# Feed-forward of a two-block transformer kernel: the up half leaves PSUM times the gate, and the norm's factor is applied to the down projection's result

## The reference

```python
def rmsnorm(x, g):
    y = x * rsqrt(mean(x * x, axis=-1) + 1e-6)       # one factor for each token
    return y * g

# first block
h2 = rmsnorm(x, norm_ffn_g[l])
x = x + (silu(h2 @ w_gate[l]) * (h2 @ w_up[l])) @ w_down[l]

# each layer of the stack
def _swiglu(x, w_in, w_out):
    gu = x @ w_in
    return (silu(gu[..., :2816]) * gu[..., 2816:]) @ w_out
x = x + _swiglu(_rmsnorm(x, g_ffn[i]), w_ffn_in[i], w_ffn_out[i])
```

## Time and profile before

| | us |
|---|---|
| median of 3 runs | 3124.99 (3124.5 to 3125.08) |
| span of the profiled execution, first to last instruction | 3122.7 |
| PE busy | 3103.8 (99%) |
| DVE busy | 1538.4 (49%) |
| ACT busy | 987.3 (32%) |
| POOL busy | 50.9 (2%) |
| mean granted clock of PE | 0.997 of full |

### The profile page before, as it was taken

One profiled execution on the slowest core, in us unless ns is written; L12 is line 12 of the kernel. 1 busy time (PEld: TensorE's weight loads), 2 busy tenths in 40 slices (PEclk: granted clock), 3 DMA queues, 4 the chain that ended last, 5 costly groups with the idle time before them and its releaser, 6 DMA issues.

```text
span 3122.7 us, 36149 instructions
## 1 busy us (share of the span) xinstructions
PE 3103.8 (99%) x14981; PEld 2572.7 (82%) x14981; DVE 1538.4 (49%) x1632; ACT 987.3 (32%) x1090; POOL 50.9 (2%) x149
## 2 busy tenths in 40 slices
PE   9999999999999999999999999999999999999998
PEld 7878888888888888888888888888888888888887
DVE  7975443464444443467544434655442454454433
ACT  3463221344442222344322222323222344332213
POOL 5100000000000000000000000000000000000000
PEclk9999999999999999999999999999999999999999
DMA  5122332342123322212322223223222321232322
GB/s 180 47 74 90 98 107 88 105 133 67 53 83 101 100 94 101 88 55 62 101 94 94 97 98 101 81 82 107 94 94 98 103 69 49 63 104 96 105 88 74
DMA packets 250513, 282.80 MB, mean 91 GB/s; under 512 B 11874, under 2 KB 216864, under 8 KB 250408
## 3 DMA queue, kind: packets, MB, share of 16 engines
q1 hardware_dynamic: 250408, 281.30, 27.9%
HBM read 279.16 MB, written 4.73 MB: 91 GB/s over the span
## 4 chain that ended last, share of the span: by engine, by line
PE 92%; DVE 4%; issue 1%; ACT 1%; POOL 1%; DMA 0%; SPq 0%; ACTq 0%; DVEq 0%
PE ps L1868 26%; PE ps L1869 26%; PE ps L1870 26%; PE ps L2436 2%; PE ps L2438 1%; PE ps L2437 1%; PE ps L2361 1%; PE ps L2372 1%; PE ps L2350 1%; DVE wlo L1157 1%; PE ps L2417 1%; PE ps L2396 1%; PE ps L2293 1%; PE ps L2313 1%; PE ps L2302 0%
## 5 line engine op out<-in xcount | busy, mean ns | idle before, releaser
L1868 PE MATMUL ps<-hh,whi 128*128 128x512 f32 x2496 | 982.5, 394 | 0.3 <-DVE wlo L1276 0.3
L1870 PE MATMUL ps<-hh,wlo 128*128 128x512 f32 x2496 | 973.1, 390 | 0.0
L1869 PE MATMUL ps<-hl,whi 128*128 128x512 f32 x2496 | 973.0, 390 | 0.0
L1157 DVE TENSOR_TENSOR wlo<-raw,whi 128x2048 fp32r<-128x2048 f32 (+2 forms) x274 | 591.1, 2157 | 632.4 <-ACT whi L689 632.0
L689 ACT ACTIVATE whi<-raw 128x2048 fp32r<-128x2048 f32 (+2 forms) x274 | 494.8, 1806 | 1141.1 <-PE ps L1870 1116.3
L1868 PEld LDWEIGHTS ps<-hh,whi 128*128 128x128 f32 x2496 | 469.0, 188 | 102.6 <-issue 4.4
L1870 PEld LDWEIGHTS ps<-hh,wlo 128*128 128x128 f32 x2496 | 468.8, 188 | 98.2
L1869 PEld LDWEIGHTS ps<-hl,whi 128*128 128x128 f32 x2496 | 469.1, 188 | 95.6 <-issue 0.7
L1868 PE MATMUL ps<-act,whi 128*128 128x512 f32 x1264 | 495.0, 392 | 1.3 <-DVE wlo L1157 0.9
L1869 PE MATMUL ps<-act,whi 128*128 128x512 f32 x1264 | 492.5, 390 | 0.0
L1870 PE MATMUL ps<-act,wlo 128*128 128x512 f32 x1264 | 492.5, 390 | 0.0
(11 more groups left out here) (396 smaller groups left out, 2438.3 us busy)
## 6 DMA issues: line engine op xcount, KB each, us to landing
raw<-in_w_ffn_in SPq DMA_DIRECT2D x88, 1024.0 KB, 5.1
raw<-in_w_in SPq DMA_DIRECT2D x59, 1024.0 KB, 5.3
raw<-in_w_ffn_out SPq DMA_DIRECT2D x40, 1024.0 KB, 5.0
raw<-in_w_o SPq DMA_DIRECT2D x32, 640.0 KB, 4.2
raw<-in_w_gate SPq DMA_DIRECT2D x11, 1024.0 KB, 5.3
raw<-in_w_up SPq DMA_DIRECT2D x11, 1024.0 KB, 5.3
raw<-in_w_down SPq DMA_DIRECT2D x10, 1024.0 KB, 5.1
raw<-in_w_mem_kv SPq DMA_DIRECT2D x8, 1024.0 KB, 5.3
```

Of the source, the lines that this page charges most:

```text
L1157: v.tensor_tensor(wlo[:, u % 2, 0:n], raw[:, u % 2, 0:n], whi[:, u % 2, 0:n].bitcast(F32), ALU.subtract).then_inc(lo_made, 1)
L1868: mm(dst, wh, xh, start=first, stop=False, skip_group_check=True)
L1869: mm(dst, wh, xl, start=False, stop=False, skip_group_check=True)
L1870: return mm(dst, wl, xh, start=False, stop=last, skip_group_check=True)
```

## The change

In a turn, DVE waits for silu and then takes the up half out of PSUM times `gs`; the pass over `us` and `gs` is gone, and so is the factor on the up half. The product that goes into the down projection is without the factor of the up half. `residual` has a new mode for the five down projections: it takes a tile out of PSUM times `rstd` into `us`, waits for that, and adds it to x.

```diff
@@ residual, DVE
                     if mode == "add":
                         ins = v.tensor_tensor(x[:, t, :], x[:, t, :], src(t), ALU.add)
+                    elif mode == "scaled":
+                        link(v.tensor_tensor(us[:, t % 2, :], src(t), rstd[:, :], ALU.mult))
+                        ins = v.tensor_tensor(x[:, t, :], x[:, t, :], us[:, t % 2, :], ALU.add)
@@ swiglu, DVE
                     dve.wait_ge(unit_used, cnt(2, u0 + 2))
+                    dve.wait_ge(silu_done, cnt(1, 11 * s + 1))
                     v.tensor_tensor(us[:, :, :], ps[:, 6 * BANK:8 * BANK].rearrange("p (a n) -> p a n", a=2),
-                                    bc(rstd[:, :], 2), ALU.mult).then_inc(acc_free, 1)
-                    dve.wait_ge(silu_done, cnt(1, 11 * s + 1))
+                                    gs[:, :, :], ALU.mult).then_inc(acc_free, 1)
+                    at_ = 2 * i if isinstance(i, int) else i * 2
                     dve.wait_ge(acc_free, cnt(2, gc + 2))
-                    v.tensor_tensor(us[:, :, :], us[:, :, :], gs[:, :, :], ALU.mult).then_inc(act_step, 1)
-                    at_ = 2 * i if isinstance(i, int) else i * 2
-                    dve.wait_ge(act_step, cnt(2, 22 * s + 1))
                     v.tensor_scalar(act2[:, bass.ds(at_, 2), 0, :], us[:, :, :], 1.0, None, ALU.mult).then_inc(act_step, 1)
-                    dve.wait_ge(act_step, cnt(2, 22 * s + 2))
+                    dve.wait_ge(act_step, cnt(1, 11 * s + 1))
                     v.tensor_tensor(act2[:, bass.ds(at_, 2), 1, :], us[:, :, :],
                                     act2[:, bass.ds(at_, 2), 0, :].bitcast(F32), ALU.subtract).then_inc(act_ready, 1)
@@ first block, and in the same way each layer
-            residual(2, lambda t: down_tile(U_DN1, 6, t), lambda t: bank(t), "add",
+            residual(2, lambda t: down_tile(U_DN1, 6, t), lambda t: bank(t), "scaled",
```

More of the change, by code:

```diff
@@ L1847, in _ @@
                 lows(u0 + L_DN + 2, u0 + L_DN + 7)
-                residual(r + 1, lambda t: down_tile(u0 + L_DN, out_tiles_before(l) + 4, t), lambda t: bank(t), "add",
+                residual(r + 1, lambda t: down_tile(u0 + L_DN, out_tiles_before(l) + 4, t), lambda t: bank(t), "scaled",
                          after={3: lambda: low(u0 + L_DN + 7)},
```

## The result

The changed kernel takes 3138.21 us (median of 5 runs, 3134.57 to 3138.83), the kernel before 3124.99: the ratio is 1.004, 95% interval 1.0028 to 1.0052. The five times lie in two groups, 3134.57 and 3134.92, and 3138.21 to 3138.83, so the median is the lowest of the upper group. The profiled execution has a span of 3136.5, so 13.8 us more than the one of before, and its own time is 3138.21, 1.7 above its span.

What follows compares the result with a forecast made beforehand. PE, busy 3103.8 of 3122.7 us, was taken to bound the kernel, so DVE counts only where PE waits. Terms 0 + 4.4 + 2.3 + 1.6 + 2.7 = 11.0 us on 3124.99 gave 3136.0, range 3131.0 to 3140.5.

Steps and rivals of the forecast that it cites:

- The turns: Dropping 55 passes over `us` and `gs`, about 67 us of DVE work, gives 0 because PE ends DVE's waits there.
- A pass: Each of 40 new tile multiplications with its linked wait costs 0.73 us on DVE, bounds 0.60 and 0.79.
- The middle of the down projections: Layers 0 to 2: multiplications of tiles 2 and 3 delay DN+7's low half by 1.46 three times: 4.4 us (3.6 to 4.7).
- Their ends: Down projections, layers 0 to 2: next layer's second unit's low half comes late, PE starts 0.76 later three times: 2.3 us.
- The end of the first block's feed-forward: Tiles 4 to 7 delay the sums, norm and low half PE waits for until 622.38: 1.57 us (1.2 to 1.7).
- The end of the program: Last tiles every 1.93 us, not 1.36, cost 1.87, plus 0.8 for the lower clock: 2.7 us (1.5 to 4.5).
- seven places: The forecast that the new passes push DVE's chains past PE at seven places, given 0.74.
- The second rival: PE's clock falls in the new gaps, once to four times, up to 3.4 us each: 3139 to 3150 us; chance 0.12.
- the clock at 0.50 between 150 and 3113 us: Sign of being wrong: PE's clock at its lower level, 1.2 GHz, anywhere between those times in the new profile.
- The rival that all is hidden: ACT's halves pace tiles 2 and 3, so only the program's end shows: 3127.7 us; chance 0.10.
- contention: Rival mechanism for a faster kernel: 39.8 us less DVE work lets matmuls run closer, 3118.8 at 0.43 each; chance 0.03.
- a hold-up by silu: Rival: silu or a counter holds the up half back; at 1 us a turn, 3191 us; chance 0.01.

Runs made afterwards that it cites:

- the turns alone: Kernel before with the changed turns and the old residual addition, the norm's factor on the up half left out: 3122.94 us against 3124.37, ratio 0.9997.
- the gap filled: Changed kernel with 12 unread transposes on PE ahead of the memory's third unit: 3135.67 us, ratio 1.004 to the kernel before.
- the tiles alone: Kernel before with its old turns and the new residual addition, the factor applied twice: 3134.91 us, ratio 1.0036.
- both moves: Changed kernel, low half of DN+7 moved behind tile 1's addition, that of the memory's third unit ahead of the norm: 3129.39 us, ratio 1.0018.
- before with both moves: Kernel before the change with the low halves of DN+7 and the memory's third unit moved earlier: 3121.73 us against 3124.55, ratio 0.999.
- the third move: Changed kernel with two low halves already moved, plus the next layer's second unit's low half ahead of tile 7's low half of h: 3131.95 us.

## Why the prediction was right

The sum was 11.0 us; 13.2 was measured, inside the range, and the traces account for 13.8 of span. Of the 13.7 by which the last matmul starts later, 11.3 stand where the sum has its terms; the other 2.4 are the clock near 620 (1.5) and the start (0.9), which it doesn't have. How near the median came to the forecast is in part luck: the lower group of the five times is 9.6 to 9.9 us above the median of before, the upper one 13.2 to 13.8.

- **The turns, 0.** Shown by the run with the turns alone: 67.2 us of DVE's work less, no change in any wait of PE behind the first 230 us.
- **A pass, 0.73.** It starts the addition 0.72 after itself. The low bound of 0.60 is excluded. The Trainium skill, "VectorE: DVE Perf Modes", section on the DRAIN, has a semaphore cost nothing extra, measured there on copies; the linked pair at 0.72 beside unlinked ones at 0.60 doesn't agree. And its rule to minimize the number of operations found 15 fewer and a longer program, because the operations that went stood under PE's cover and those that came did not.
- **The middle of the down projections, 4.4.** Measured 1.45 + 1.44 + 1.44 = 4.3. Shown twice over: moving one low half takes the waits away, and doubling the passes adds 1.71 to each.
- **Their ends, 2.3.** Measured 0.76 + 0.71 + 0.71 = 2.2. That PE waited for the low half is shown by moving it. That ACT's high half between tiles 6 and 7 makes the chain is read from the timeline, not tried.
- **The end of the first block's feed-forward, 1.6.** Measured 1.5, split in two waits as said, 1.1 and 1.8. By the prediction's own bound of 0.79 for a pass its upper end is 1.8, not 1.7.
- **The end of the program, 2.7.** Measured 3.3: 1.9 for the tiles as worked out, and 1.4 where I took 0.8 for the lower clock. This term came out larger because three of the four groups of small matmuls fell behind the clock's fall: they grew from 0.95 to 1.26, from 1.03 to 1.84 and from 1.69 to 1.95. No fixed size would have been right: with the same tiles the part of the clock was 0.4 us in the trace with the gap filled, 1.6 in the second one of the changed kernel and 2.5 in that of the low half of DN+7 placed earlier, all between the bounds of 0 and 2.6 that the prediction gave it.
- **The number of places.** The prediction speaks of seven places; its terms have eight, three middles, three ends, the first block's end and the program's, and all eight showed.
- **The second rival came true once.** The clock fell near 620 and took 1.5 us. The prediction had it at 0.12 and apart from the forecast, and it named the clock at 0.50 between 150 and 3113 us as a sign of being wrong. This sign appeared: the waits were right, and a cost that hangs on them was missing from the sum. It should have been a term.
- **What goes with that fall.** All six traces in which it fell have the wait for the sums. In three of them (the tiles alone, the passes twice, the low half of the next layer moved) it fell 1.2 to 2.3 us after PE had started again behind that wait, before PE came to the third unit. In the other three (the changed kernel twice, the low half of DN+7 moved) it fell 0.7 to 1.0 us after PE had started again behind the wait of 1.8 at the third unit. In the last three traces with the wait for the sums it didn't fall; the wait at the third unit was gone there (the memory's low half moved, both moves) or 0.5 us (the gap filled). In the three traces without the wait for the sums (before, the turns alone, before with both moves) it never fell, although PE waited 1.6 at the third unit in two of them. So the wait for the sums goes with every fall, and the second wait isn't needed. That the two together make it likelier is what these counts suggest, in one to three traces of each kind; what decides in a single execution stays open.
- **0.9 at the start** has nothing to do with the change: in the profiles of one and the same program the stretches at the lower clock in the first 150 us differ.

The rival that all is hidden fell with the waits of the middle, contention and a hold-up by silu with the turns alone.

## What to carry to other kernels

When one engine is 99% busy, count an edit on another engine not by its work but by where it stands: list the points at which the busy engine resumes on something of that engine's, take the slack there, and push the new instructions through. Fusing where the engine waits anyway is worth nothing, and a pass moved into the handful of places where its results are urgent costs its full length each time once the slack there is used up, however few passes there are: in the middle of a down projection two of the four passes went into DVE's pause, and the other two showed whole. Where such a chain also carries work for later (here the low half of the next weights), placing that work in a pause ahead of the urgent part takes the wait away at no cost; place by place, check what it makes late, since the third move made tile 7 late.

## What the hardware showed unexpectedly

The change moves the program by 13 us, and the executions of one kernel differ by 4 to 5 us in themselves: the kernel before took 3121.86 to 3126.12 us in 15 runs on one chip, and 3122.55 to 3127.35 in 23 on another. Beside the end of the program, the profiles show stretches of 3.4 or 6.8 us at the clock's lower level, near 137 us in nine of the twelve. Effects of one or two microseconds are therefore read from the starts of the same matmul in two traces, where they agree to 0.1 us (1.96 and 1.96, 0.87 and 0.87 in two executions), and not from medians of five.

And short stops of an otherwise dense PE can cost more than their length. Behind stops of 1.1 and 1.8 us, with 4.0 us of matmuls between them, 3.4 us ran at half the clock in both traces of the changed kernel, 1.5 us lost. In the trace with the tiles alone the clock fell 2.3 us after the first of these stops had ended; there the slow stretch ran into the second one, which shrank from 1.83 to 0.50, and nothing was lost. The stops of 1.57 us in the middle of the down projections were never followed by such a stretch; those of 3.28 us, in the kernel with the passes twice, were in all three layers.
